# Opening of a diffusion backbone: tokens and parameters by channel, adaptive groups that serve two channel tiles each, adaptive weights in 8 KB rows

## The reference

```python
silu_c, silu_cc = silu(c), silu(c_ctx)                 # (1, 1024), (1024,)
mod_x = silu_c  @ ada_w[i] + ada_b[i]                  # ada_w[i] is 1024 x 6144
mod_c = silu_cc @ ada_w[i] + ada_b[i]
sx1, cx1, gx1, sx2, cx2, gx2 = split(mod_x, 6)         # shift, scale, gate, twice
hx = rmsnorm(x,   norm1_g[i]) * (1 + cx1) + sx1        # 512 tokens
hc = rmsnorm(ctx, norm1_g[i]) * (1 + cc1) + sc1        # 256 tokens
z = h @ conv_pw1_w + conv_pw1_b                        # 1024 -> 2048
a, g = split(z, 2)
u = dwconv31(a * sigmoid(g))                           # depthwise over tokens
u = silu(layernorm(u)) @ conv_pw2_w + conv_pw2_b
```

## Time and profile before

| | |
|---|---|
| runs | 1671.04, 1672.41, 1673.03 us; median 1672.41 |
| profiled execution | the page gives its span from first to last instruction, 1670.0 us |
| TensorE | busy 98% of the span |
| DVE, ACT, POOL | busy 57%, 41%, 10% |
| chain that ended last | TensorE 84%, DVE 12%, DMA 1%, ACT 1% of the span |
| granted TensorE clock, mean | 0.996 |

### The profile page before, as it was taken

The page is one execution under the profiler, slowest core; times in us unless marked ns, Lnnn a source line. Parts: engine busy times, 40 slices in busy tenths (PEclk is TensorE's granted clock), DMA queues, the critical chain, the costliest instruction groups (busy, mean ns, idle before and its releaser), DMA issues.

```text
span 1670.0 us, 25612 instructions
## 1 busy us (share of the span) xinstructions
PE 1642.8 (98%) x10058; PEld 1437.3 (86%) x10058; DVE 955.4 (57%) x1511; ACT 679.5 (41%) x1023; POOL 169.4 (10%) x180
## 2 busy tenths in 40 slices
PE   6999989999999999999999999999999999999998
PEld 4777759998888888888899999999999888888888
DVE  6899987763424342334358665656566754543444
ACT  4656667642323222223245333424244543333334
POOL 2488851000000000000000000000000000000000
PEclk9999999999999999999999999999999999999999
DMA  9777742221221212121213221312122324333321
GB/s 338 253 252 251 252 158 96 77 74 50 67 76 54 71 55 72 54 72 53 60 51 92 63 70 39 83 51 63 58 64 76 99 79 122 89 104 89 100 88 52
DMA packets 238032, 165.67 MB, mean 99 GB/s; under 512 B 5288, under 2 KB 213016, under 8 KB 237944
## 3 DMA queue, kind: packets, MB, share of 16 engines
q1 hardware_dynamic: 234088, 150.43, 29.8%
q0 software_dynamic: 2992, 10.88, 2.0%
q10 hardware_dynamic: 864, 3.15, 0.5%
HBM read 162.34 MB, written 2.10 MB: 98 GB/s over the span
## 4 chain that ended last, share of the span: by engine, by line
PE 84%; DVE 12%; DMA 1%; ACT 1%; issue 1%; DVEq 0%; POOL 0%; ACTq 0%
PE ps L707 83%; DVE ps L1914 3%; DVE ps L1931 3%; DVE w_lo L1710 2%; DMA ada<-in_ada_w 1%; DVE H_lo L1751 1%; PE ps L921 0%; DVE rstd L1716 0%; DVE tmp L1739 0%; DVE ps L1929 0%; DVE sq L1739 0%; DVE ps L1911 0%; DMA conv<-in_x 0%; DVE sq L2016 0%; DVE tap_even L1935 0%
## 5 line engine op out<-in xcount | busy, mean ns | idle before, releaser
L707 PE MATMUL ps<-H_hi,w_hi 128*128 128x512 f32 (+1 forms) x1712 | 583.5, 341 | 7.5 <-DVE H_lo L1813 5.0
L707 PE MATMUL ps<-H_lo,w_hi 128*128 128x512 f32 (+1 forms) x1712 | 579.6, 339 | 0.0
L707 PE MATMUL ps<-H_hi,w_lo 128*128 128x512 f32 (+1 forms) x1712 | 578.9, 338 | 0.0
L707 PEld LDWEIGHTS ps<-H_hi,w_hi 128*128 128x128 f32 x1712 | 325.6, 190 | 60.9 <-issue 23.4
L707 PEld LDWEIGHTS ps<-H_hi,w_lo 128*128 128x128 f32 x1712 | 325.6, 190 | 35.0
L707 PEld LDWEIGHTS ps<-H_lo,w_hi 128*128 128x128 f32 x1712 | 325.8, 190 | 34.3
L1710 DVE TENSOR_TENSOR w_lo<-w_raw,w_hi 128x1024 fp32r<-128x1024 f32 x208 | 255.0, 1238 | 107.7 <-ACT w_hi L1246 74.8
L707 PE MATMUL ps<-mid_hi,w_hi 128*128 128x512 f32 (+1 forms) x592 | 199.4, 337 | 0.6
L707 PE MATMUL ps<-mid_lo,w_hi 128*128 128x512 f32 (+1 forms) x592 | 198.3, 335 | 0.0
L707 PE MATMUL ps<-mid_hi,w_lo 128*128 128x512 f32 (+1 forms) x592 | 198.1, 335 | 0.0
L2242 DVE SCALAR_TENSOR_TENSOR tmp<-ps,par,tmp 128x511 f32<-128x511 f32 x66 | 41.6, 658 | 231.3 <-ACT tmp L1595 155.0
(11 more groups left out here) (284 smaller groups left out, 2100.1 us busy)
## 6 DMA issues: line engine op xcount, KB each, us to landing
w_raw<-in_ffn_w_in SPq DMA_DIRECT2D x88, 512.0 KB, 3.9
ada<-in_ada_w SPq DMA_DIRECT2D x40, 1024.0 KB, 6.2
w_raw<-in_ret_w_in SPq DMA_DIRECT2D x40, 512.0 KB, 3.9
w_raw<-in_ffn_w_out SPq DMA_DIRECT2D x32, 512.0 KB, 4.4
w_raw<-in_conv_pw_w SPq DMA_DIRECT2D x22, 512.0 KB, 8.8
w_raw<-in_ffn_w_out SPq DMA_DIRECT2D x16, 384.0 KB, 3.5
ada<-in_ada_w POOLq DMA_DIRECT2D x4, 1024.0 KB, 13.7
w_raw<-in_ret_w_out SPq DMA_DIRECT2D x8, 512.0 KB, 4.2
```

The costliest lines, as they stand in the source:

```text
L707: return nc.tensor.matmul(o, a, b, start=first, stop=last, skip_group_check=True)
```

## The change

The token and parameter loads, the statistics and the grouping of the first adaptive weights are written anew.

- The host gives the tokens by channel (`x_cols`), the parameters as one array of 128 x 768 (`params`), and `ada_w` as 24 groups of two halves, laid out so that a partition's share of a half is one run of 8 KB (`ada_groups`). Before, it was four runs of 2 KB. Which numbers are computed stays the same.
- SP's queue loads the parameters in one transfer, then `X` in four transfers of two tiles, straight into place. The token and parameter transposes and `bn_stats` are gone.
- The sums of squares come from ACT (`Square` of each tile) and TensorE, which multiplies each of six token blocks of a squared tile, as the stationary operand, with one column of `mean_of`: 48 products of one column.
- Each of the first four groups holds shift and scale of two channel tiles: group m serves tiles 2m and 2m + 1. `first_modulation` runs four times.
- The streams of TensorE, ACT and DVE are written in rounds by group.
- POOL issues its loads once the second pair of tiles has landed, with the gate unit's weights between groups 0 and 1.

The core of the diff:

```diff
-FIRST_GROUPS = [0, 2, 1, 3]
+FIRST_GROUPS = 4
+            sp.dma_start(par[:], params).then_inc(par_in, 16)
+            for n in range(KT // 2):
+                sp.dma_start(X[:, 2 * n:2 * n + 2, :], x_cols[:, 2 * n:2 * n + 2, :]).then_inc(x_in[n], 16)
+            sp.dma_start(ident[:], eye).then_inc(eye_in, 16)
...
             def load_first(eng, m, half):
-            rows = slice(half * D // 2, (half + 1) * D // 2)
-            g = FIRST_GROUPS[m]
-            eng.dma_start(ada_first[m][half], ada_w[0][rows, g * GROUP * P:(g + 1) * GROUP * P]
-                          .rearrange("(k p) n -> p k n", p=P)).then_inc(ada_first_in[m], 16)
+            eng.dma_start(ada_first[m][half], ada_groups[m, half].rearrange("p (k n) -> p k n", n=GROUP * P)) \
+                .then_inc(ada_first_in[m], 16)
...
 # TensorE
+            pe.wait_ge(filled, 1)
+            for k in range(KT):
+                pe.wait_ge(x_squared, k + 1)
+                for t in range(6):
+                    m = mm(tok_sums[:, t:t + 1], norm_buf[k % 4][:, t * P:(t + 1) * P], mean_of[:, 0:1],
+                           k == 0 and t == 0, k == KT - 1)
+                m.then_inc(x_summed, 1)
             pe.wait_ge(diag_ready, 1)
             mm(ps[:, 3, :], mean_of[:], flat_sq[:, LATS], True, True)
             mm(ps[:, 4, 0:CTX], mean_of[:], flat_sq[:, CTXS], True, True).then_inc(rows_ready, 1)
+            ada_products(0)
+            ada_transposes(0)
-            first_block(0, 0, 1)
+            first_block(0, 0, 2)
+            ada_products(1)
+            ada_transposes(1)
+            first_block(1, 0, 2)
+            first_block(0, 2, 4)
             ada_products(2)
-            first_block(0, 1, 3)
             ada_transposes(2)
-            first_block(0, 3, 4)
+            first_block(1, 2, 4)
+            first_block(0, 4, 6)
             ada_products(3)
-            first_block(1, 0, 1)
             ada_transposes(3)
-            first_block(1, 1, 4)
-            first_block(0, KT // 2, KT - 2)
+            first_block(1, 4, 6)
             ada_products(4)
-            first_block(0, KT - 2, KT)
-            first_block(1, KT // 2, KT)
+            first_block(0, 6, KT)
+            first_block(1, 6, KT)
             ada_transposes(4)
...
 # ACT
+            for k in range(KT):
+                act.wait_ge(x_in[k // 2], 16)
+                if k >= 4:
+                    act.wait_ge(x_summed, k - 3)
+                A(norm_buf[k % 4], X[:, k, :], ACT.Square).then_inc(x_squared, 1)
+            act.wait_ge(x_summed, KT)
+            A(tok_rstd[:], tok_sums, ACT.Sqrt, bias=eps[:, 0:1]).then_inc(tok_std, 1)
...
 # DVE
-            normed_rows(range(KT // 2))
-            dve.wait_ge(par_ready, 2)
-            ada_sum(1, 0, FIRST_GROUPS[1])
-            first_modulation(2, 0)
-            first_shifted(0)
-            split_lo(0, 0)
-            first_lo(0)
-            first_tiles(range(1, KT // 2))
-            split_lo(1, 1)
-            normed_rows(range(KT // 2, KT))
-            ada_sum(2, 0, FIRST_GROUPS[2])
-            ada_sum(3, 0, FIRST_GROUPS[3])
-            first_modulation(4, 1)
-            first_tiles(range(KT // 2, KT))
+            normed_rows(range(KT))
+            for m in range(FIRST_GROUPS):
+                ada_sum(m, 0, m)
+                first_modulation(m)
+                if m < 2:
+                    first_shifted(2 * m)
+                    split_lo(m, m)
+                    first_lo(2 * m)
+                    first_tiles([2 * m + 1])
+                else:
+                    first_tiles([2 * m, 2 * m + 1])
```

More of the change, by code:

```diff
@@ L76, in tail_uses @@
     return FULL + (KT - FULL) * parts
-S_XT = 0
-S_PW1 = S_XT + 12
+S_PW1 = 0
 S_LN = S_PW1 + 2 * KT
@@ L327, in backbone @@
         ages_in = sem("ages_in")
-        tokens_in = [sem("tokens_in0"), sem("tokens_in1"), sem("tokens_in2")]
+        x_in = [sem(f"x_in{n}") for n in range(KT // 2)]
         ada_first_in = [sem(f"ada_first_in{g}") for g in range(4)]
@@ L891, in ada_products @@
                     pe.wait_ge(ada_row_ready, m)
-                first = isinstance(m, int) and m < 4
+                first = isinstance(m, int) and m < FIRST_GROUPS
                 for half in range(2):
@@ L911, in ada_transposes @@
                 o.then_inc(ada_T, 1)
[L914 to L943, removed]
+            pe.wait_ge(filled, 1)
[5 more added lines that the diff above has]
+                m.then_inc(x_summed, 1)
             pe.wait_ge(diag_ready, 1)
-            pe.wait_ge(slot_read[1], S_PW1 // 2)
             mm(ps[:, 3, :], mean_of[:], flat_sq[:, LATS], True, True)
             mm(ps[:, 4, 0:CTX], mean_of[:], flat_sq[:, CTXS], True, True).then_inc(rows_ready, 1)
-            ada_products(1)
-            ada_transposes(1)
+            pe.wait_ge(silu_c_ready, 2)
+            pe.wait_ge(eye_in, 16)
+            ada_products(0)
+            ada_transposes(0)
             def first_block(h, k0, k1):
@@ L1784, in modulation, with first_modulation @@
                             .then_inc(mod_ready, 1)
[L1787 to L1790 removed]
+            def first_modulation(m):
+                dve.wait_ge(mod_sum, m + 1)
+                js = slice(2 * m, 2 * m + 2)
                 rows = par[:, ADA_B:ADA_B + 2 * KT].rearrange("p (a j) -> p a j", a=2)[:, :, js]
[L1792 to L1796 removed]
+                cols = mod[:, 0, 4 * m:4 * m + 4, :].rearrange("p (a j) c -> p a j c", a=2)
+                v.tensor_tensor(cols, cols, rows.unsqueeze(3).to_broadcast([P, 2, 2, 2]), ALU.add).then_inc(mod_ready, 1)
+                dve.wait_ge(mod_ready, 2 * m + 1)
+                v.scalar_tensor_tensor(gain[:, 0, 0, js, :], mod[:, 0, 4 * m + 2:4 * m + 4, :], 1.0,
+                                       two(par[:, NORM1 + 2 * m:NORM1 + 2 * m + 2]), ALU.add, ALU.mult) \
                     .then_inc(mod_ready, 1)
[L1798 removed]
+                dve.wait_ge(mod_ready, 2 * m + 2)
             def first_shifted(j):
@@ L2442, in _, with laid_out, columns @@
             ffn(FFN1, S_FFN1, 1, False, X_FFN1)
-_INS = ["x", "c", "ctx", "c_ctx", "ada_w", "ada_b", "norm1_g", "norm2_g", "conv_pw1_w", "conv_pw1_b", "conv_dw_w",
-        "conv_dw_b", "conv_ln_g", "conv_ln_b", "conv_pw2_w", "conv_pw2_b", "ret_w_in", "ret_w_out", "ret_decay_f",
-        "ret_decay_b", "ret_gn_f", "ret_gn_b", "ffn_w_in", "ffn_dw_w", "ffn_dw_b", "ffn_w_out", "final_g"]
+_PLAIN = ["conv_pw1_w", "conv_pw2_w", "ret_w_in", "ret_w_out", "ret_decay_f", "ret_decay_b", "ret_gn_f", "ret_gn_b",
+          "ffn_w_in", "ffn_w_out"]
+def laid_out(inputs):
+    import numpy as np
+    def columns(name):
+        return np.asarray(inputs[name]).reshape(-1, P).T
+    params = np.zeros((P, 768), np.float32)
+    for at, name in ((ADA_B, "ada_b"), (NORM1, "norm1_g"), (NORM2, "norm2_g"), (PW1_B, "conv_pw1_b"), (DW_B, "conv_dw_b"),
+                     (LN_G, "conv_ln_g"), (LN_B, "conv_ln_b"), (PW2_B, "conv_pw2_b"), (FFN_DW_B, "ffn_dw_b"),
+                     (FINAL_G, "final_g"), (C_COL, "c"), (C_COL + KT, "c_ctx"), (DW_W, "conv_dw_w")):
+        rows = columns(name)
+        params[:, at:at + rows.shape[1]] = rows
+    taps = columns("ffn_dw_w").reshape(P, DEPTH, 3 * FT)
+    for layer in range(DEPTH):
+        params[:, FFN_DW_W + P * layer:FFN_DW_W + P * layer + 3 * FT] = taps[:, layer]
+    tokens = np.concatenate([np.asarray(inputs["x"])[0], np.asarray(inputs["ctx"])[0]])
+    x_cols = np.ascontiguousarray(tokens.reshape(TOK, KT, P).transpose(2, 1, 0))
+    w = np.asarray(inputs["ada_w"])
+    first = w[0][:, 0:2 * D].reshape(D, 2, FIRST_GROUPS, 2 * P).transpose(0, 2, 1, 3).reshape(D, 2 * D)
+    both = np.concatenate([first, w[0][:, 2 * D:], w[1]], axis=1)
+    groups = np.ascontiguousarray(both.reshape(2, KT // 2, P, 24, GROUP * P).transpose(3, 0, 2, 1, 4)
+                                  .reshape(24, 2, P, KT // 2 * GROUP * P))
+    return [("x_cols", x_cols), ("params", params), ("ada_groups", groups)]
 def shape_constants():
```

145 lines of the change are left out of this document (32 added, 113 removed).

## The result

The changed kernel took **1700.5 us** (median of 4 runs, 1697.45 to 1701.2), the kernel before 1672.52 (4 runs, 1671.04 to 1673.03) beside it on the same chip. The ratio is 1.0165, 95% interval 1.0153 to 1.0177: slower by 28 us, and 0.5 us beyond the upper end of the predicted range. The profiled execution spans 1699.4 us, 29.4 more than before.

A forecast was written before the change was run, and what follows sets the result against it. Bytes and DVE together bounded the opening, which sets the convolution's start; TensorE is 98% busy. Start -0.4, order and handoffs +13.1, tail +2.1, clock +2.5 gave +17.3 us, 1689.7; range 1681 to 1700.

The forecast's parts named there:

- T, end of the token sums: Moment when the last token sum on TensorE is ready: taken as 20 us, between 17.7 and 26.
- T to the first normalized tile: From the token sums' end to DVE's first normalized tile: 3.7 us, as before, so DVE starts at 23.7.
- tiles, to the first group sum: All eight normalized tiles on DVE stand ahead of the first adaptive sum: 7.1 us.
- three handoffs: DVE idle between a round's last `H_lo` and the next group's sum, waiting for TensorE: 5.1 us each, 15.3 in all.
- last `H_lo` to L1932: From the opening's last `H_lo`, T + 44.9, through group 4 and gate unit to the convolution's start, T + 53.7.
- clock, as a term of its own: Low TensorE clock after waits: 1.5 us in the first round, 1.0 ahead of the value unit's `w_lo`; 2.5 together.
- T = 26: Upper bound for the token sums' end: 96 passes at 0.2 us, 19 us.
- half-hidden rival (3): Handoffs half hidden, or T 17.7 and group 4 quick: +4 to +11 us, 1676 to 1683; chance 0.07.
- faster one (2): Bytes decide in the opening and the handoffs are hidden, so DVE's work alone counts: 1669 us; chance 0.06.
- The tail: Opening's end: TensorE waits for late-issued group 4 ahead of the last two tiles, then gate unit; +2.1 us.
- rival (1): Clock stays low through all rounds, T may be 26: +28 to +34 us, 1700 to 1706; chance 0.08.
- Bytes: Longer rows can bring the adaptive groups sooner; costed at nothing, since only group 4 is waited for.

The follow-up runs named there:

- b: Changed kernel with eight extra, unused 512-column products on TensorE ahead of the token sums (b_warm); 1697.22 us, ratio 1.0158.
- a: Changed kernel with the squared tiles added on DVE, so TensorE does 6 one-column products instead of 48; 1688.14 us, ratio 1.0095.
- e: Changed kernel with the adaptive groups' products moved ahead of the products with H on TensorE, ACT's copies matched; 1680.09 us, ratio 1.0051.
- c: Changed kernel, its loads and TensorE token sums kept, with the order of before (two rounds of four tiles) put back; 1684.88 us, ratio 1.0076.
- h: Changed kernel with the order of before put back and the sums of squares added on DVE as well; 1673.91 us, ratio 1.0012.
- d: Kernel before, with its adaptive weights alone packed in rows of 8 KB; 1674.03 us, ratio 1.0014.

## Why the prediction missed

The direction and the main mechanism were right. The step that failed is the first one, the token sums: the sum has them end at 20 us, and they ended at 27.6. The forecast of +17.3 was 11.2 short of the +28.5 at the start of the convolution, and 7.6 of that is this term. By the prediction's own terms:

| step | predicted | measured | missing |
|---|---|---|---|
| T, end of the token sums | 20 | 27.6 | 7.6 |
| T to the first normalized tile | 3.7 | 4.9 | 1.2 |
| tiles, to the first group sum | 7.1 | 7.0 | 0 |
| three handoffs | 15.3 | 17.4 | 2.1 |
| last `H_lo` to L1932 | 8.8 | 11.6 | 2.8 |
| clock, as a term of its own | 2.5 | (in the rows above) | -2.5 |

**The token sums: the term that was mis-sized.** The prediction named the pace of a low clock, 0.2 us a pass, but let it last for 5 us only, because the transposes had gone so for that long, and charged 0.11 after that. TensorE's timeline of the changed kernel, and the window over the sums (busy of PE, PEld, DVE, ACT, POOL):

```profile
6.98 5.25 PE L682 MATMUL ps<-mean_of,tmp 128*128 128x1 f32 x24 [6.98 <-ACT tmp L1267]
12.10 5.26 PE L682 MATMUL ps<-mean_of,sq 128*128 128x1 f32 x24
17.22 5.26 PE L682 MATMUL ps<-mean_of,tmp 128*128 128x1 f32 x24
22.34 5.26 PE L682 MATMUL ps<-mean_of,sq 128*128 128x1 f32 x24
...
7.00:27.60 20.60, 20.59 (x96) 20.51 (x96) 0.00 (x0) 6.80 (x8) 5.11 (x8) 1.00 0.97 369
```

All 96 passes go at 0.21 us, 20.6 us with no idle time: half the clock from first to last (`b` has this very pace, 5.26, where its window shows 0.50). The 1.00 in the window is no recorded clock, as the last section says. Loading weights (PEld) is busy for 20.51 of the 20.60 us too: each pass has its own weights. The upper bound that the prediction gave, T = 26, was made with 0.2 a pass and 7.1 as start and was itself 1.6 too low. `a` took the sums away and gave 9.8 us of T back; with this term at its measured size the sum would have been +24.9, 1697.3, inside the range. The transposes were the wrong neighbour. In the kernel before they go at 0.22 us a pass from 9.10, and a little later at 0.15:

```profile
14.66 1.17 PE L921 MATMUL ps<-ident,conv 128*128 128x128 f32 x8
```

So the clock rose while they ran, and it did not rise while the one-column products ran.

The Trainium skill ("TensorE: Matmul & The Clock Gate", section "What's actually happening") says that the throttled state is the default and activity releases it. This case's rows agree on the start of the program; they add that the clock stayed low while 96 one-column passes ran without a gap, and that it fell again in `b_warm` among such passes.

**The rest of the way to the tiles.** The prediction took 3.7 us from before, where the row sums (two products, four passes) took 1.53 us: here they take 2.93. It charged the clock only from the first round on.

**The handoffs: right.** Three waits of 5.8, 6.7 and 5.0 us stand before the second to fourth sum, all released by TensorE's transposes. `e` took them away by order alone and gained 20.0 us (17.8 up to the last `H_lo`, where 17.4 had been waiting, and 2.2 behind it); `c` and `h` confirm it with the other order. The 2.1 us above the 15.3 predicted are those of a low clock, below. The half-hidden rival (3) and the faster one (2) needed handoffs that DVE could fill, and it had nothing to fill them with.

**The tail: right in mechanism, 2.8 us too small.** TensorE waited for group 4 as predicted, and the gate unit's last products then came at half clock, which the sum had not charged there. The timeline of TensorE (idle before, and what ended it, in brackets):

```profile
74.59 1.06 PE L682 MATMUL ps<-ada,silu_c 128*32 128x512 f32 x8 [0.80 <-DMA ada<-in_ada_groups]
77.94 1.93 PE L682 MATMUL ps<-ada,silu_c 128*32 128x512 f32 x8 [2.29 <-DMA ada<-in_ada_groups]
79.80 0.80 PE L682 MATMUL ps<-H_hi,w_hi 128*128 128x512 f32 x1
80.39 0.63 PE L682 MATMUL ps<-H_lo,w_hi 128*128 128x512 f32 x1
80.82 0.63 PE L682 MATMUL ps<-H_hi,w_lo 128*128 128x512 f32 x1
```

Eight passes took 1.06 us at 74.59 and 1.93 at 77.94, and the products behind come every 0.43 us instead of 0.23. Against the predicted steps, group 4's second half landed 0.6 us late, its products took 0.9 longer and the gate unit's 2.1 longer, and what follows the gate unit took 0.8 less.

**The clock.** The changed kernel's windows by the granted clock:

```profile
39.80:46.50 6.70, 3.24 (x7) 2.16 (x8) 4.92 (x9) 2.50 (x4) 0.00 (x0) 0.50 0.17 71
46.70:53.40 6.70, 3.27 (x27) 1.39 (x26) 2.70 (x7) 3.72 (x6) 0.00 (x0) 1.00 0.00 0
53.50:56.80 3.30, 3.30 (x11) 2.72 (x11) 2.33 (x4) 0.22 (x1) 0.00 (x0) 0.50 0.00 0
77.40:84.10 6.70, 6.16 (x21) 3.93 (x22) 1.21 (x9) 0.61 (x2) 0.00 (x0) 0.50 1.10 380
```

It fell three times: in 7.24 us without work ahead of the first products with `H`, at the first products of the value unit (2.72 us without work ahead of them), and in the tail, around the wait for group 4. Between 56.9 and 77.2 us it was full. The handoffs' excess (2.1), group 4's products (0.9) and the gate unit's end (2.1) together are 5.1 us, against the 2.5 that the sum held. So rival (1) was half right: its T of 26 or more and the tail's share of its clock term came, its slow rounds did not all come, and the time fell just inside its lower end (1700), where the forecast's range stops. It had been given 0.08. It tied together two things that are separate: low clock in the sums, where no other work stands, and low clock in the rounds.

**Bytes: costed at nothing, and near it.** In the changed kernel DMA moves 122 GB/s through the rounds, and `d` shows that longer rows alone don't make the kernel before faster. Only group 4 is waited for, and its second half took 7.51 us from issue to landing, where the sum had 7.2.

## What to carry to other kernels

Before two steps of a kernel are brought closer together (here shift and scale of the same tiles), look at what each engine has to do between handing on and getting back; a work item that looked badly placed may have been what filled that gap. The repair costs no work: put the products that start a chain ahead of those that can wait, and give the waiting engine something of its own. Where a reduction is moved to TensorE as many products of one column, price it from a row at the low clock for its whole length, and ask for each term of a sum which clock its row was taken at.

## What the hardware did that was not expected

- One-column products with 128 x 128 weights, issued without a gap for 20.6 us, never raised TensorE's clock, and in `b_warm` the granted clock fell from 1.00 to 0.50 in the midst of them. The profile calls both stretches fully busy. One pass took 0.11 us at 2.4 GHz and 0.21 at 1.2.
- The window over the sums of the changed kernel gives a granted clock of 1.00, though the passes have the pace of 0.50. The clock's record has its first entry at 32.95, a rise, and what lies ahead of a first entry is shown as full speed. There the pace of a known instruction is the better witness. The Trainium skill ("TensorE: Matmul & The Clock Gate", the caveats on the clock's trace in the section "Seeing it yourself") warns that the clock's events can be unreliable. Here the changes on record agree with the passes' pace (1.93 us for eight passes at 77.94, where the window shows 0.50, and 1.06 at 74.59); what is missing is the state ahead of the first.
- In the kernel before, packing the adaptive weights in 8 KB rows brought the groups 0.6 to 0.9 us sooner (medians of SP's and POOL's) and one small load beside them 5.3 us later.
